# A two-layer hybrid decoder trunk on one core: first norm by plain transposes and a broadcast row of scales, transposed merge and gates, output in four banks, head 0 picked in halves, last two rows on VectorE

## The chip, the core and the metric
The kernel runs on one core of one Trainium2 chip. The metric is the device time of one launch in microseconds. Before the change it is 1635.47 us, the median of 3 runs (1634.2 to 1636.94). All data is float32.

## The reference
256 tokens of 1024 channels go through two equal layers and a last RMSNorm. A layer is:

```python
h = rmsnorm(x, g_mix)
p, q, k, v, gl = split(h @ w_in)                  # 512 | 512 | 512 | 512 | 2048
branch_a = pool_mixer(p, w_pool, pool_scale)      # trailing means over 2/4/8/16 tokens, minus the token,
                                                  # 4 groups of 128 channels mapped to 256 each, times pool_scale
o = moba_attention(q, k, v)                       # one block of 256: causal attention with ALiBi, 8 heads of 64
branch_b = o @ w_attn_up
gates = sigmoid(gl)
x = x + (gates[:1024] * branch_a + gates[1024:] * branch_b) @ w_out
x = x + peer_ffn(rmsnorm(x, g_ffn), ...)
```

`peer_ffn`: queries `xc @ w_q` (8 heads of 2 x 128), scores against 2 x 128 sub keys, the best 16 of each half, the best 16 of their 256 sums; so each token has 8 x 16 = 128 experts. Expert e adds `softmax weight * gelu(u[e] . xc) * v[e]`. The rows u[e] and v[e] lie side by side in one table `uv` (16384 per layer, 2048 floats each).

## The kernel before
**Tiles and windows.** The work is cut into four windows w = 0 to 3: layer w // 2, tokens of tile w % 2 (128 tokens, one a partition). Each window has two parts. The *mix* (`tensor_mix`, `scalar_mix`, `vector_mix`) is everything up to the choice of the experts: norm, projections, pooling, attention, gates, output projection, second norm, queries, scores and top 16. The *stream* is 64 ticks of two expert rows: GpSimd gathers one row per token (128 x 8 KB = 1 MB) into one of 8 ring slots; VectorE takes the dot product with `tok` (`dot`, L855); ScalarE makes the GELU weight and a diagonal matrix of it (`scalar_tick`, L667 to L692); TensorE adds diag @ v into two banks (`tensor_tick`, L514), or VectorE adds the row itself (`weighted`, L869). A slot is free for the next gather when its row is added.

**Order.** There is one hand-written order. `streamed` runs, on each engine, tick t of the stream and then the pieces of the mixes that are due at t; a mix piece says when with `yield when(w, n)`, which is tick 64 (w - 1) + 4 + n. So the mix of w + 1 runs inside the stream of w, and the mix of window 0 runs before tick 0, with nothing to stream. An engine executes its list in order and waits on semaphores in it.

**Weights.** They come in 30 chunks of 1 MB a window (`chunks`), issued by SyncE in order: C_Q and C_K (2 each), C_V, C_P (2 each), C_GATE (8), C_UP (2), C_OUT (4), C_PQ (8, one per PEER head). Chunks C_UP to the first of C_PQ are held in SBUF for both windows of a layer (`held`), the other 23 go through three slots (`wring`); SyncE waits until the chunk three before is used. In a tick in which a chunk of the next mix is due (`takes_chunk`), TensorE adds only row 1 and VectorE adds row 0. In window 0's own mix the chunks of the eight heads' queries are due at ticks -19, -17, ... -5.

**Banks.** Six PSUM banks are taken in turn by `claim(name, reader)`; TensorE waits until the bank six claims before has been read.

**The norm.** `squares` (ScalarE, L533), `inverse_mean` (VectorE, L707 and L709) and `root` (ScalarE, L537) give 1/rms per token; ScalarE turns it into a diagonal `rinv_diag` (L580); TensorE multiplies x by it, which transposes and scales at once (L391), and ScalarE copies the blocks to `hT` with the gain of each channel (`turned`, L544). Keys and gains arrive as rows and are transposed on TensorE (L384, L385).

**Pooling, gates, merge, output.** `everywhere` (L309) spreads a row of gains over all partitions; for `pool_scale` VectorE multiplies `wpool` by it (L802). `rows_by` (L355) makes results with the tokens on the partitions, `cols_by` (L373) with the channels. Gates, pooling and `up` (L470) have tokens on the partitions, so `merged` is made by VectorE (L810, L817, L821), transposed on TensorE (L328), copied by ScalarE (L524), and only then multiplied with the C_OUT chunks (L355) into two banks, which VectorE adds to x (L825). Then x is transposed again (L328) and copied with the second gain (L544).

**Heads.** For each head: queries (L373), copy (L524), scores (L493), copy, then on VectorE `key_search` (L722, L725, L728), `sum_search` (L738 to L749), `pick` (L755 to L766) and `weigh_heads` (L772, L774). GpSimd waits for `expert_ready` of a head before its first gather, `hand_over` (L847) makes `tok` at tick 0 of a window. After the last tick come `close` (L877) and the last norm of tile 1 (L895, L899, L908).

Of the kernel before, what the change touches and what calls it, by code (L numbers as in the profile page):

```python
# [20 lines left out]
P = 128  # L21
# [49 lines left out]
HEAD_LOADS = 5  # L71
# [10 lines left out]
G_MIX, G_FFN, G_POOL, G_FINAL = 0, KC, 2 * KC, 3 * KC  # L82
G_ROWS = 4 * KC
# [34 lines left out]
def build(nc, consts, chunks, uv, x, mix_norm, w_pool, pool_scale, ffn_norm, peer_keys, final_norm, out):  # L118
    depth = mix_norm.shape[0]
    windows = depth * NT  # L120

    with ExitStack() as ctx:
# [13 lines left out]
        gainT = sb("gainT", [P, 2, KC])  # L136
        wpool = sb("wpool", [P, NG, GOUT])
        keysT = sb("keysT", [P, 2, NK])
# [9 lines left out]
        rinv_diag = sb("rinv_diag", [P, P])  # L148
# [24 lines left out]
        keys = buf2[:, D:D + 2 * P].rearrange("p (a n) -> p a n", a=2)  # L173
# [20 lines left out]
        heads_in = sem("heads_in")  # L194
# [8 lines left out]
        rinv_diag_done = sem("rinv_diag_done")  # L203
# [18 lines left out]
        normed_done = sem("normed_done")  # L222
# [12 lines left out]
        def when(w, tick):  # L235
# [3 lines left out]
        first_heads = [(-10, -8, -6), (-2, -1, 1), (2, 3, 5), (7, 9, 10), (12, 13, 15), (17, 18, 20), (21, 23, 24),  # L239
                       (26, 27, 29)]  # L240

# [7 lines left out]
        takes_chunk = {when(w, n) for w in range(1, windows) for n in CHUNK_TICKS}  # L249

        def rows_on_tensor(t):

            return (1,) if t in takes_chunk else (0, 1)

# [58 lines left out]
        def tensor_mix(pe, w):  # L313
# [10 lines left out]
            def turn(name, half, src):  # L324
                b = claim(f"{name}{half}", a_done)
                for j in range(4):
                    lo = (4 * half + j) * P
                    ins = pe.transpose(b[:, j * P:(j + 1) * P], src[:, lo:lo + P], ident)  # L328
                filled(f"{name}{half}", ins)
# [13 lines left out]
            def due(c):  # L343
                return when(w, CHUNK_TICKS[c])
# [16 lines left out]
            def cols_by(c, name, n):  # L361
# [3 lines left out]
                for m in range(n):  # L365
# [4 lines left out]
                    for half in range(2):  # L370
                        lo = half * P
                        for k in range(KC):
                            ins = pe.matmul(b[:, m * CW + lo:m * CW + lo + P], wt[:, k, lo:lo + P], hT[:, k, :],  # L373
                                            start=(k == 0), stop=(k == KC - 1))
                freed[w, c + n - 1] = filled(name, ins)

            yield when(w, 3)
            if w == 0:
                pe.wait_ge(ident_in, 16)
            if tile == 0:  # L380
                pe.wait_ge(heads_in, 16 * HEAD_LOADS * (layer + 1))
                b = claim("heads", a_done)
                for a in range(2):
# [646 lines left out]
```

## Time and profile before
| what | value |
|---|---|
| median of 3 runs | 1635.47 us (1634.2 to 1636.94) |
| the profiled execution's own time | 1631.79 us |
| its span | 1630.0 us |
| busy PE / DVE / ACT / POOL | 1335.7 / 1078.0 / 772.2 / 615.3 us |
| moved by DMA | 653.33 MB, mean 401 GB/s |
| expert rows / weight chunks | 512 x 1 MB / 106 x 1 MB |
| mean granted TensorE clock | 0.957 |

The page gives each engine's busy time, the span in 40 equal slices, the DMA queues, the chain of work that ended last, and the costliest groups of instructions. PE is TensorE's matmul, PEld its weight load, DVE VectorE, ACT ScalarE, POOL GpSimd, SP SyncE; "L391" is line 391 of the kernel. A float32 product is recorded as two passes, so a query chunk of 16 products of 128 x 128 stands as x32; a transpose is one pass. The wait tables name for each idle time of an engine what ended it.

### The profile page before, as it was taken

What the parts mean: (1) busy time and instruction counts of PE and PEld (TensorE: products, weight loads), DVE (VectorE), ACT (ScalarE), POOL (GpSimd) and SP (SyncE); (2) the same over time, 40 slices, a digit from 0 to 9 for tenths busy, and PEclk for the clock granted to TensorE, in tenths of its full rate; (3) what the DMA queues carried; (4) which work ended last, traced back from release to release, by engine and by line L of the source; (5) the groups of instructions that cost most, each with busy time, mean ns of one, the idle gap of its engine ahead of it and who ended that gap; (6) DMA issues with size and microseconds to landing.
All of it is one profiled execution on the core that took longest, in us unless ns stands there. A gap on an engine that the chain in (4) does not pass through costs nothing.

```text
span 1630.0 us, 16753 instructions
## 1 busy us (share of the span) xinstructions
PE 1335.7 (82%) x4974; PEld 785.1 (48%) x4974; DVE 1078.0 (66%) x2539; ACT 772.2 (47%) x2882; POOL 615.3 (38%) x516
## 2 busy tenths in 40 slices
PE   8987878889878788877888888897988877778776
PEld 7876455535554265533454436563555422233322
DVE  0135879766678677755567787867656876777544
ACT  2223635445545544424554463544564555555554
POOL 0002432345434332323543343334543444554551
PEclk9998999999999898988999899999999999999999
DMA  7849999999999999999999999999999999999996
GB/s 290 305 183 387 412 423 410 424 422 414 421 423 411 423 402 423 422 426 417 416 420 423 415 400 410 423 423 422 415 422 422 413 421 421 421 413 421 402 421 250
DMA packets 91963, 653.33 MB, mean 401 GB/s; under 512 B 10144, under 2 KB 11872, under 8 KB 12768
## 3 DMA queue, kind: packets, MB, share of 16 engines
q0 software_dynamic: 73728, 536.90, 79.7%
q1 hardware_dynamic: 18144, 115.36, 17.4%
q8 instruction: 39, 0.64, 0.2%
q14 instruction: 52, 0.43, 0.1%
HBM read 651.17 MB, written 1.05 MB: 400 GB/s over the span
## 4 chain that ended last, share of the span: by engine, by line
DMA 51%; PE 19%; DVE 15%; issue 7%; ACT 5%; POOL 3%; another core or an unknown queue 0%; DVEq 0%; ACTq 0%; POOLq 0%
DMA ring<-in_uv,expert 50%; PE ybank L514 10%; DVE ring L855 6%; PE bank L373 3%; PE bank L355 3%; DVE xs L869 3%; POOL ring L953 3%; ACT wgt L681 1%; ACT diag L692 1%; ACT half_p L669 1%; ACT th L675 1%; DVE buf L758 1%; DVE picked L761 1%; DVE ci L728 1%; DVE buf L755 1%
## 5 line engine op out<-in xcount | busy, mean ns | idle before, releaser
L514 PE MATMUL ybank<-ring,diag 128*128 128x512 f32 x1688 | 834.1, 637 | 268.6 <-ACT diag L692 266.9
L953 POOL DMA_INDIRECT ring<-in_uv,expert x512 | 615.1, 1201 | 989.5 <-DVE xs L869 413.6
L855 DVE SCALAR_TENSOR_TENSOR ring<-ring,tok 128x1024 f32<-128x1024 f32 x512 | 620.4, 1224 | 402.9 <-DMA ring<-in_uv,expert 398.5
L514 PEld LDWEIGHTS ybank<-ring,diag 128*128 128x128 f32 x1688 | 317.6, 198 | 704.2 <-ACT diag L692 378.5
L667 ACT ACTIVATE sq<-dots 128x2 f32<-128x2 f32 x256 | 52.2, 204 | 704.7 <-DVE ring L855 704.7
L355 PE MATMUL bank<-wring,hT 128*128 128x256 f32 x768 | 178.1, 387 | 0.3 <-DMA wring<-in_chunks 0.3
L681 ACT ACTIVATE wgt<-th,half_p 128x1 f32<-128x1 f32 x512 | 170.1, 379 | 8.6
L355 PEld LDWEIGHTS bank<-wring,hT 128*128 128x128 f32 x768 | 150.8, 197 | 41.5 <-issue 21.3
L373 PEld LDWEIGHTS bank<-hT,wring 128*128 128x128 f32 x1408 | 164.7, 195 | 7.4 <-issue 5.7
L373 PE MATMUL bank<-hT,wring 128*128 128x128 f32 x1408 | 167.1, 278 | 1.2 <-ACT hT L544 1.2
L692 ACT ACTIVATE diag<-cst,wgt 128x128 f32<-128x128 f32 x422 | 149.8, 392 | 5.4
L669 ACT ACTIVATE half_p<-dots,prob 128x1 f32<-128x1 f32 x512 | 119.1, 280 | 0.0
L869 DVE SCALAR_TENSOR_TENSOR xs<-ring,wgt,xs 128x1024 f32<-128x1024 f32 x90 | 115.3, 1281 | 0.3 <-ACT wgt L681 0.3
L675 ACT ACTIVATE th<-arg,dots 128x1 f32<-128x1 f32 x256 | 75.4, 294 | 8.2
L672 ACT ACTIVATE arg<-sq,gelu_bias 128x2 f32<-128x2 f32 x256 | 71.9, 281 | 0.0
L676 ACT ACTIVATE th<-arg,dots 128x1 f32<-128x1 f32 x256 | 71.3, 279 | 0.0
L355 PE MATMUL bank<-held,hT 128*128 128x256 f32 x256 | 57.5, 379 | 0.7 <-ACT hT L524 0.7
L355 PEld LDWEIGHTS bank<-held,hT 128*128 128x128 f32 x256 | 48.6, 190 | 12.7 <-issue 5.7
L524 ACT ACTIVATE buf<-bank 128x256 f32<-128x256 f32 (+1 forms) x64 | 27.3, 448 | 55.0 <-PE bank L355 25.3
L855 DVE DVE_READ_ACCUMULATOR ring<-ring,tok 128x1 f32 x512 | 42.2, 82 | 0.0
L728 DVE FIND_INDEX8 si<-sv,buf 128x8 uint32<-128x128 f32 x128 | 34.9, 285 | 0.0
L725 DVE MAX8 sv<-buf 128x8 f32<-128x128 f32 x128 | 31.0, 284 | 5.4 <-ACT buf L524 4.3
(101 smaller groups left out, 702.0 us busy)
## 6 DMA issues: line engine op xcount, KB each, us to landing
wring<-in_chunks SPq DMA_DIRECT2D x92, 1024.0 KB
held<-in_chunks SPq DMA_DIRECT2D x14, 1024.0 KB, 17.3
ring<-in_uv,expert POOLq DMA_INDIRECT x512
xs<-in_x SPq DMA_DIRECT2D x2, 512.0 KB, 11.3
wpool<-in_w_pool SPq DMA_DIRECT2D x2, 512.0 KB, 14.0
trunk_out<-buf SPq DMA_DIRECT2D x4, 256.0 KB, 4.7
cst<-in_consts SPq DMA_DIRECT2D x1, 672.0 KB, 8.0
buf<-in_peer_keys SPq DMA_DIRECT2D x2, 128.0 KB
```

Of the source, the lines that this page charges most:

```text
L355: ins = pe.matmul(b[:, m * CW:(m + 1) * CW], hT[:, k, :], wt[:, k, :], start=(k == 0), stop=(k == KC - 1))
L373: ins = pe.matmul(b[:, m * CW + lo:m * CW + lo + P], wt[:, k, lo:lo + P], hT[:, k, :], start=(k == 0), stop=(k == KC - 1))
L514: ins = pe.matmul(ybank[m][:, :], diag[:, nth % DIAGS, :], ring[:, (2 * t + r) % RING, D + m * BANK:D + (m + 1) * BANK], start=(nth == ten ...
L669: act.activation(half_p[:, c:c + 1], dots[:, c:c + 1], ACT.Copy, scale=prob[:, w % 2, 2 * n + r:2 * n + r + 1])
L672: act_stepped(act.activation(arg[:, :], sq[:, :], ACT.Identity, scale=0.044715 * GELU_C, bias=gelu_bias[:, 0:1]))
L675: act.activation(th[:, 0:1], arg[:, 0:1], ACT.Tanh, scale=dots[:, col[0]:col[0] + 1])
L676: act_stepped(act.activation(th[:, 1:2], arg[:, 1:2], ACT.Tanh, scale=dots[:, col[1]:col[1] + 1]))
L681: ins = act.activation(wgt[:, c:c + 1], th[:, r:r + 1], ACT.Identity, scale=half_p[:, c:c + 1], bias=half_p[:, c:c + 1])
L692: act.activation(diag[:, nth % DIAGS, :], ident, ACT.Copy, scale=wgt[:, col[r]:col[r] + 1]).then_inc(diag_done, 1)
L855: dve.scalar_tensor_tensor(out=ring[:, g % RING, 0:D], in0=ring[:, g % RING, 0:D], scalar=1.0, in1=tok[:, :], op0=ALU.mult, op1=ALU.mult, ...
L869: dve.scalar_tensor_tensor(out=total, in0=ring[:, 2 * t % RING, D:2 * D], scalar=wgt[:, c:c + 1], in1=total, op0=ALU.mult, op1=ALU.add).th ...
L953: pool.indirect_dma_start(ring[:, g % RING, :], None, uv, bass.IndirectOffsetOnAxis(ap=expert[:, w % 2, at:at + 1], axis=0)).then_inc(row_ ...
```

## The change
- Mixing norm: TensorE transposes x as it is (no scaling), as soon as x is there. When 1/rms is ready, one product of `stat` broadcast over 128 columns with the identity gives a bank whose every row holds all tokens' scales; VectorE copies it (`rinv_all`) and makes `hT` with 8 `scalar_tensor_tensor` (block x gain x scale). ScalarE's `rinv_diag` and its 8 copies go. The first chunk's products wait for `hT` in two halves.
- Keys and gains come already transposed in one array (`side`, by `beside`); their transposes and copies go. In the SyncE list of window 0 chunk 0 is now ahead of them. `gains` has 3 rows of gains.
- `pool_scale` of layer 0 is a broadcast DMA into ring slot 0 (512 KB written), and VectorE multiplies `wpool` in one instruction; layer 1 still uses `everywhere`.
- Gates by `cols_by`, pooling and `up` with channels on the partitions, so `merged` is born transposed: its 8 transposes and 2 copies go. The factor 0.5 moves to the addition to x.
- Output in four banks of 256 columns, each added to x on its own tick (33 to 36). In window 0 the first four blocks of x are transposed ahead of the last C_OUT chunk.
- Window 0, head 0: query and score by side (a, b), the search of side a beside the product of side b; the squares of the second norm on VectorE; the 16 experts are picked in two halves of 8, and GpSimd starts after the first.
- Window 0's queries of heads 5, 6 and 7 move to ticks 0, 2 and 4; in these ticks row 0 goes to VectorE. `sum_search(1)` moves from tick -1 to tick 0; the weight of head 0 is made after `key_search(1)`.
- Last tick: both rows are added by VectorE, ScalarE makes their weights one after the other; the tensor sum is added ahead of the last row.
- Last norm: VectorE multiplies by the gain ahead of the root; then ScalarE scales columns 0 to 511 and VectorE the rest.

```diff
@@ order of window 0's queries
+        first_queries = (-19, -17, -15, -13, -11, 0, 2, 4)
+        def query_tick(w, h):
+            return when(w, CHUNK_TICKS[C_PQ + h]) if w else first_queries[h]
-        takes_chunk = {when(w, n) for w in range(1, windows) for n in CHUNK_TICKS}
+        takes_chunk = {when(w, n) for w in range(1, windows) for n in CHUNK_TICKS} | set(first_queries)
         def rows_on_tensor(t):
+            if t == windows * TICKS - 1:
+                return ()
             return (1,) if t in takes_chunk else (0, 1)
@@ tensor_mix: the norm
-            pe.wait_ge(rinv_diag_done, w + 1)
-            for half in range(2):
-                b = claim(f"h{half}", a_done)
-                for j in range(4):
-                    lo = (4 * half + j) * P
-                    ins = pe.matmul(b[:, j * P:(j + 1) * P], x_of(tile)[:, lo:lo + P], rinv_diag[:, :],
-                                    start=True, stop=True)
-                filled(f"h{half}", ins)
-            yield due(C_Q)
-            pe.wait_ge(*read(w, "h1"))
+            turn("h0", v_done, 0, 4)
+            turn("h1", v_done, 4, 4)
+            pe.wait_ge(root_done, 2 * w + 1)
+            b = claim("rinv", rinv_copied)
+            filled("rinv", pe.matmul(b[:, 0:P], stat[:, 0, 2:3].to_broadcast([P, P]), ident, start=True, stop=True))
@@ tensor_mix: head 0 of window 0
+            def first_query():
...
+                pe.wait_ge(x_mixed, OUTS * w + OUTS - 1)
+                g = claim("g2", a_done)
+                a = claim("pq0a", a_done)
+                side(0, a, range(6))
+                pe.wait_ge(x_mixed, OUTS * w + OUTS)
+                for j in range(2):
+                    ins = pe.transpose(g[:, j * P:(j + 1) * P], x_of(tile)[:, (6 + j) * P:(7 + j) * P], ident)
+                filled("g2", ins)
+                pe.wait_ge(*read(w, "g2"))
+                filled("pq0a", side(0, a, range(6, KC)))
+                a_scores, b = claim("score0a", a_done), claim("pq0b", a_done)
+                side(1, b, range(4))
+                scores(0, a_scores)
+                freed[w, C_PQ] = filled("pq0b", side(1, b, range(4, KC)))
+                scores(1, claim("score0b", a_done))
@@ tensor_mix: merge and output
-            yield when(w, 29)
-            pe.wait_ge(merged_done, 2 * (w + 1))
-            turn("merged", 0, merged)
-            turn("merged", 1, merged)
-            yield due(C_OUT)
-            pe.wait_ge(*read(w, "merged1"))
-            yield from rows_by(C_OUT, "out0", v_done)
-            yield from rows_by(C_OUT + 2, "out1", v_done)
+            for n in range(OUTS):
+                if w == 0 and n == OUTS - 1:
+                    turn_mixed(0)
+                yield due(C_OUT + n)
+                wt, b = weights(C_OUT + n), claim(f"out{n}", x_mixed)
+                for k in range(KC):
+                    if n == 0 and k % 4 == 0:
+                        pe.wait_ge(merged_done, 2 * w + k // 4 + 1)
+                    ins = pe.matmul(b[:, 0:CW], mergedT[:, k, :], wt[:, k, :], start=(k == 0), stop=(k == KC - 1))
+                freed[w, C_OUT + n] = filled(f"out{n}", ins)
@@ vector_mix: the norm
+            yield when(w, 4)
+            if tile == 0:
+                dve.wait_ge(side_in, 16 * (layer + 1))
+            dve.tensor_copy(rinv_all[:, :], bank("rinv")[:, 0:P]).then_inc(rinv_copied, 1)
+            dve.wait_ge(*read(w, "rinv"))
+            for half in range(2):
+                b = bank(f"h{half}")
+                for j in range(4):
+                    k = 4 * half + j
+                    ins = dve.scalar_tensor_tensor(out=hT[:, k, :], in0=b[:, j * P:(j + 1) * P],
+                                                   scalar=gainT[:, 0, k:k + 1], in1=rinv_all[:, :],
+                                                   op0=ALU.mult, op1=ALU.mult)
+                ins.then_inc(v_done, 1)
@@ the last tick and the last norm
+        def close_last(dve):
+            w, t = windows - 1, windows * TICKS - 1
+            weighted(dve, t, 0).then_inc(dve_summed, 1)
+            dve.wait_ge(dve_summed, vector_rows(t) + 1)
+            dve.wait_ge(pe_summed, tensor_rows(t))
+            for m in range(2):
+                step(sum_of_tensor(dve, w, m))
+            settle(dve)
+            weighted(dve, t, 1).then_inc(x_final, 2)
...
+            act.activation(normed(tile)[:, 0:BANK], normed(tile)[:, 0:BANK], ACT.Copy,
+                           scale=stat[:, tile, 2:3]).then_inc(normed_a, 1)
...
+            dve.tensor_scalar(normed(tile)[:, BANK:D], normed(tile)[:, BANK:D], stat[:, tile, 2:3], None,
+                              ALU.mult).then_inc(normed_v, 1)
@@ gathers and SyncE's list
-                    if at % TOPK == 0:
-                        pool.wait_ge(expert_ready, PH * w + at // TOPK + 1)
+                    if g == 0:
+                        pool.wait_ge(expert_ready, 1)
+                    elif g == 8:
+                        pool.wait_ge(expert_ready, 2)
+                    elif at % TOPK == 0:
+                        pool.wait_ge(expert_ready, experts_of(w, at // TOPK))
...
+                        if tile == 0 and c == (1 if w == 0 else 0):
+                            heads(layer)
                         chunk(w, c)
...
+                            if layer == 0:
+                                sp.dma_start(ring[:, 0, 0:D], pool_scale[0:1, :].to_broadcast([P, D])
+                                             ).then_inc(scale_in, 16)
```

## Rows read from the trace of the kernel before

**Rows 1.** The page: DMA share in tenths and GB/s in 40 slices.
```profile
DMA  7849999999999999999999999999999999999996
GB/s 290 305 183 387 412 423 410 424 422 414 421 423 411 423 402 423 422 426 417 416 420 423 415 400 410 423 423 422 415 422 422 413 421 421 421 413 421 402 421 250
```

**Rows 2.** Stretches of the whole core: length, busy (count) by engine, clock, DMA share, GB/s.
```profile
95.00:111.00 16.00, 13.86 (x96) 12.50 (x95) 3.06 (x15) 4.27 (x13) 0.00 (x0) 1.00 0.01 3
...
155.00:160.00 5.00, 5.00 (x10) 2.13 (x9) 4.83 (x21) 3.73 (x14) 1.88 (x2) 0.78 0.38 123
...
200.00:1600.00 1400.00, 1144.40 (x4012) 642.97 (x4011) 991.66 (x2287) 691.10 (x2625) 582.02 (x484) 0.96 1.01 418
```

**Rows 3.** Chain that ended last, window 0's mix: start us, us, what.
```profile
6.29 3.80 PE bank L391 x16
...
10.11 1.15 ACT hT L544 x4
...
11.31 11.00 PE bank L373 x96
22.32 7.26 DMA wring<-in_chunks
...
49.44 1.98 PE bank L309 x16
...
76.16 6.88 PE bank L470 x16
...
86.44 14.08 PE bank L355 x64
...
100.99 2.19 ACT hT L544 x8
...
103.22 3.85 PE bank L373 x32
```

**Rows 4.** VectorE's instructions from head 0's search to its pick.
```profile
108.85 0.49 DVE L725 MAX8 sv<-buf 128x8 f32<-128x128 f32 x2 [4.26 <-ACT buf L524]
...
118.44 0.17 DVE L766 TENSOR_SCALAR expert<-picked 128x16 uint32<-128x16 f32 x1
```

**Rows 5.** Groups of VectorE instructions by shape, whole run.
```profile
L786 DVE SCALAR_TENSOR_TENSOR buf<-cst,bank 128x128 f32<-128x128 f32 x16 | 3.8, 280 | 28.6 <-PE bank L406 28.6
...
L869 DVE SCALAR_TENSOR_TENSOR xs<-ring,wgt,xs 128x1024 f32<-128x1024 f32 x90 | 115.3, 1281 | 0.3 <-ACT wgt L681 0.3
```

**Rows 6.** GpSimd's gathers: start, us, [idle before <- what ended it].
```profile
118.90 1.08 POOL L953 DMA_INDIRECT ring<-in_uv,expert  x1 [118.44 <-DVE expert L766]
...
127.74 1.30 POOL L953 DMA_INDIRECT ring<-in_uv,expert  x1 [0.30 <-issue]
156.55 0.94 POOL L953 DMA_INDIRECT ring<-in_uv,expert  x1 [27.50 <-PE ybank L514]
```

**Rows 7.** Waits in 118 to 135 us, the longest of ScalarE.
```profile
ACT buf L524 <- remote: 6.9, 1, 6.9
```

**Rows 8.** A stretch of the mix of window 1 inside stream 0, columns as in rows 2.
```profile
260.00:270.00 10.00, 7.14 (x21) 4.18 (x20) 9.76 (x24) 4.17 (x18) 2.23 (x2) 0.84 1.02 420
```

**Rows 9.** The last ticks and the end, all engines in order of time.
```profile
1603.29 1.74 POOL L953 DMA_INDIRECT ring<-in_uv,expert  x1 [0.76 <-PE ybank L514]
...
1614.18 3.70 PE L514 MATMUL ybank<-ring,diag 128*128 128x512 f32 x8 [1.27 <-ACT diag L692]
...
1615.39 1.23 DVE L855 SCALAR_TENSOR_TENSOR ring<-ring,tok 128x1024 f32<-128x1024 f32 x1 [1.23 <-DMA ring<-in_uv,expert]
...
1619.12 3.70 PE L514 MATMUL ybank<-ring,diag 128*128 128x512 f32 x8 [1.24 <-ACT diag L692]
...
1622.92 1.29 DVE L877 TENSOR_TENSOR xs<-xs,ybank 128x512 f32<-128x512 f32 x2 [6.30 <-PE ybank L514]
1624.24 1.06 ACT L895 ACTIVATE buf<-xs 128x1024 f32<-128x1024 f32 x1 [3.38 <-DVE xs L877]
...
1626.05 1.41 DVE L908 SCALAR_TENSOR_TENSOR buf<-xs,stat,bank 128x512 f32<-128x512 f32 x2 [0.27 <-ACT stat L899]
```

More of the change, by code:

```diff
@@ L375, in cols_by, with side, scores @@
                 freed[w, c + n - 1] = filled(name, ins)
+            def first_query():
+                wt = weights(C_PQ)
+                def side(r, b, ks):
+                    for k in ks:
+                        ins = pe.matmul(b[:, 0:P], wt[:, k, r * P:(r + 1) * P], hT[:, k, :],
+                                        start=(k == 0), stop=(k == KC - 1))
+                    return ins
+                def scores(r, b):
+                    pe.wait_ge(*read(w, f"pq0{'ab'[r]}"))
+                    filled(f"score0{'ab'[r]}", pe.matmul(b[:, 0:NK], pqT[:, r, :], keysT[:, r, :],
+                                                         start=True, stop=True))
+                pe.wait_ge(x_mixed, OUTS * w + OUTS - 1)
[13 more added lines that the diff above has]
+                scores(1, claim("score0b", a_done))
             yield when(w, 3)
@@ L485, in tensor_mix @@
+            yield when(w, 37)
+            if w:
+                turn_mixed(0)
+            turn_mixed(1)
+            if w:
+                turn_mixed(2)
             yield due(C_PQ)
             pe.wait_ge(*read(w, "g1"))
-            for h in range(PH):
+            if tile == 0:
+                pe.wait_ge(side_in, 16 * (layer + 1))
+            if w == 0:
+                first_query()
+            else:
+                pe.wait_ge(*read(w, "g2"))
+            for h in range(0 if w else 1, PH):
@@ L488, in tensor_mix @@
                 yield from cols_by(C_PQ + h, f"pq{h}", 1)
-                yield when(w, 43 + 2 * h)
+                if w == 0 and h == 1:
+                    pe.wait_ge(gains_in, 16)
+                    everywhere(pe, w, G_FFN, "gain")
+                yield query_tick(w, h) + 2
                 pe.wait_ge(*read(w, f"pq{h}"))
@@ L495, in tensor_mix @@
                 filled(f"score{h}", ins)
-                if w == 0 and h == 1:
-                    everywhere(pe, w, G_FFN, "gain")
             if w:
@@ L620, in scalar_mix @@
             yield when(w, 30)
-            for half in range(2):
-                copy_out(f"merged{half}", hT[:, 4 * half:4 * half + 4, :], scale=0.5)
             if w == 0:
```

383 lines of the change are left out of this document (228 added, 155 removed).

## The prediction
> **What bounds the kernel now.** I read the slices first [rows 1]. There are two regimes. In the first three slices (to 122 us) DMA moves 290, 305 and 183 GB/s; from the fourth on it stays near 420 with a busy share of 9 tenths, to the last slice. The stretches say the same more finely [rows 2]: 200 to 1600 us runs at 418 GB/s with a DMA share of 1.01, while TensorE is busy 1144 of 1400 us and VectorE 992. So the stream is bound by transfers: 512 rows and the chunks must pass, and what an engine saves in it is worth nothing by itself. Between 95 and 111 us DMA stands still (share 0.01): everything that fits is loaded, and no expert is known yet. The first gather goes at 118.90, released by the experts of head 0 [rows 6]. So what counts is (1) how early the gathers begin, (2) idle DMA after that, (3) the time from the last row's landing (1615.39, when VectorE's wait for it ends [rows 9]) to the end of the span, 1630.0: 14.6 us.
>
> In the chain [rows 3] the reader is to see that window 0's mix is bound by TensorE, with short stops in which another engine works on what TensorE waits for. Those stops are what the change goes for. I take the sum against the profiled execution (span 1630.0, its own time 1631.79, which is 3.7 under the median 1635.47) and move the difference to the median.
>
> **First norm.** Before, the first projection starts at 11.31: x scaled on TensorE from 6.29 to 10.09, four copies on ScalarE, start [rows 3]. After, the eight transposes need only x and the identity and lie beside the squares on ScalarE; the root is done at about 5.8 (the diagonal's use starts at 6.29, 0.45 behind it). Then one product (2 passes, 0.5), a copy and 4 VectorE instructions on 128 x 128 from a bank. Such a one takes 280 ns alone [rows 5], about 0.24 in a series: 1.3 for the first half, so TensorE could start at 7.7, and the second half comes 1.0 later, beside 8 passes of the first products. That saves 3.6. Against it: VectorE first waits for `side`, which SyncE issues behind 1.6 MB of x and chunk 0; at the rates of the start that is near 7.0 to 7.5, so the start moves to about 8.5. And TensorE: its 16 passes at 6.29 took 3.80, 0.237 each, the 96 from 11.31 on 11.00, 0.115 each [rows 3]: it works at half speed until it has worked a while, that is at 1.2 of its two levels 1.2 and 2.4 GHz. The new kernel gives it less to do before the first projection, so part of chunk 0 may run slow: up to 1.8 (half of its 3.6). Bounds: saves 0.3 to 3.6; I take 2.0.
>
> The Trainium skill ("TensorE: Matmul & The Clock Gate", Part 1) says the same of it: the throttled clock is the default and activity releases it. The row agrees (0.237 against 0.115); by that rule alone the saving would be 3.6 - 0.8 - 1.8 = 1.0 and not 2.0, which is the second rival below.
>
> **Scale of the pool.** `everywhere` for it stands in the chain with 1.98 [rows 3]; in layer 0 it goes. VectorE's multiplication lies beside gate chunks. The broadcast DMA writes 0.5 MB at a time when SyncE's chunks are just in time (chunk 5 took 7.26 from issue to use [rows 3]): 0.5 MB at 0.42 MB/us is 1.2. Bounds: saves 0.8 to 2.0; I take 2.0: the chunks of 30 to 95 us have room, DMA stands still from 95 on [rows 2].
>
> **Up to output.** `up` ends at 83.04 (76.16 + 6.88) and the output product starts at 86.44 [rows 3]: 3.4 of VectorE, transposes and copies. After, the first half of `merged` is ready 1.5 after `up0`, so under `up1`; the second is ready 1.5 after `up1`, while the first four blocks of out0 take 8 passes of 128 x 256, 1.8 (16 such passes are a chunk, 3.5). Nothing is left of the stop: 3.3 saved, bounds 2.9 to 3.4. The same products as channels by tokens cost as much (32 passes at 0.112 against 16 at 0.22). Four transposes of x go ahead of the last output chunk: +0.6.
>
> So the last output product ends at 100.5 - 2.0 - 2.0 - 3.3 + 0.6 = 93.8.
>
> **From there to the first gather.** Before: 118.9 - 100.5 = 18.4: 2.7 to the query product (ScalarE's 8 copies, 2.19), 3.85 for it [rows 3], copies and scores to 108.85, search and pick to 118.44 (9.8) [rows 4]. After, counted from the end of the last output product E: g1 copied, TensorE goes on at E + 1.15; 12 passes 1.35; two transposes and copies, E + 3.9; 4 passes, a copy (4.7), 8 passes of side b meanwhile, score a and its copy E + 5.9; search a 1.8, E + 7.7. Side b: passes, copy, score, copy, also E + 7.7; search b, E + 9.5. Sums 0.55, best 8 and places 1.45, pick of 8: six instructions of 128 x 128 at 0.31 and two small, 2.25; E + 13.7, and 0.4 to GpSimd: 14.1. Saved 4.3; bounds 2 (copies and waits pile up) to 5.5. First gather at about 107.9, 11.0 earlier.
>
> **What lies behind it.** Moving the gathers does not move all bytes. The chunk of head 4 (1 MB), loaded by 118.9 before, is now issued only 3 ahead of the first gather: +1.5. The stream then starts with 8 rows and 4 chunks, some 28 us of transfer. Before, TensorE did the queries of heads 5 to 7 first; no slot came free until 156.55 [rows 6], and DMA ran dry: share 0.38 in 155 to 160 [rows 2], 3.5 with its edges. After, TensorE reaches tick 0 at about 119.5 (five queries, the gain bank) and the first slots come free at 124: cover 107 to 134, so 10 to spare, and the dry stretch goes: -3.5. The spare also covers ScalarE's one odd wait of 6.9 [rows 7], should it return. Bounds 0 to 3.5.
>
> **In the stream.** VectorE gets more: three rows for heads 5 to 7 (3 x 1.28 [rows 5]); in each mix a copy, 8 instructions (2.3) and, new, a wait for TensorE. Behind that wait in VectorE's list are the dots of the next tick. VectorE is a tick ahead: TensorE ends tick 3 about 6.8 after its dots (ScalarE 3, TensorE 3.7), the transposes and the product add 1.6, so VectorE waits 3.4 and is back 5.7 later, 3.3 behind the rows. A gather issued at 1603.29 is used at 1615.39 [rows 9], 12.1 later, of which a row's own transfer is 2.5 and the fixed part about 2: 7.6 of slack. It holds. But in window 0's stream VectorE has places without any (9.76 busy of 10 [rows 8]). Bounds 0 to 6; I take 2, nearer to the slack of rows 9. What ScalarE and TensorE lose there is worth 0.
>
> Last row used at 1615.4 - 11.0 + 1.5 - 3.5 + 2.0 = 1604.4.
>
> **The end.** Before, from the landing L: dot 1.25, ScalarE, TensorE 3.7 from L + 3.7, sums (1622.92), squares, root, two products with the gain, the second ready at L + 12.1, output [rows 9]. After: TensorE's last work is tick 254's, L - 1.2 + 3.7 = L + 2.5; sums 1.3; last row on VectorE 1.25: L + 5.1 against L + 8.8. Its weight is there at L + 2.6. Squares 1.2 beside 1.4 of gain, inverse 0.4, root 0.2, then 0.6 on ScalarE beside VectorE: L + 7.9; output 2.5 and 0.4 for a second issue: 10.8 instead of 14.6, -3.8, bounds 2.5 to 4.5.
>
> **Sum.** -11.0 + 1.5 - 3.5 + 2.0 - 3.8 = -14.8: span 1615.2, median 1635.5 - 14.8 = 1620.7.
>
> **Rivals.**
> 1. VectorE or TensorE sets the pace of the first 150 us of stream 0 and the early start runs into full slots: the 3.5 stay and the stream costs 6 instead of 2, -7.3: 1628.2. For it: VectorE at 9.76 of 10 [rows 8]. Against: DMA share 1.02 in that same row.
> 2. The first projection runs at 1.2 GHz for its first 3.6 (the passes of 0.237 in rows 3): the start gives 1.0 instead of 2.0, 1621.7.
> 3. Slower: VectorE's new wait isn't covered. Place: tick 4 of each mix in the stream; price: 5.7 in each of three windows, 17.1, and the three added rows 3.8: 20.9 in the place of my 2.0, 1639.6. It decides once the slack of 7.6 falls under 3.3. Against: rows 9's own gap.
> 4. The change does no more than shift the gathers: chunks that could be loaded early are behind them, and in place of 1.5 the first rows share DMA with 4 chunks until VectorE starves: 5 of the 11.0 is lost, 1625.7.
> 5. Everything goes to its good bound (3.6, 5.5, no loss in the stream, 4.5): 1615.2.
>
> **Chances.** Forecast 0.47, rival 1 0.16, rival 2 0.12, rival 3 0.05, rival 4 0.11, rival 5 0.09. The range of 8 in 10 is 1613.5 to 1629.0. A measurement of this kernel can tell some 0.2% (3.3 us) from no change. Faster by more: 0.90 (all but rival 3 and the tail of rival 1); within it 0.05; slower 0.05.
>
> **What would show it.** The first product of the first projection at 8 to 9 us; the output product right behind `up`; no `everywhere` before 100; the first gather at 106 to 110; DMA share above 0.95 in every 5 us from 110 on; tick 0's first product at 120 to 124; last landing to end 11. I am wrong if DMA runs dry in the first 60 us of the stream or the rate in the stream falls under 415.

## The result and the profile after
The changed kernel takes 1620.24 us (median of 4, 1619.65 to 1624.07) against 1634.84 (median of 4, 1632.85 to 1636.94); the ratio is 0.9919 [0.9908, 0.9931]. 1620.7 was forecast. The number is right and part of its sum is not: the start gave less than half of what I counted (5.2 of 11.0), and executions of one kernel differ by more (up to 8 us) than the error of 5.8 that this left.

The first two fences are the page of the changed kernel, its two lines of 40 slices, and stretches of it (length, busy by engine, clock, DMA share, GB/s), to be laid beside [rows 1] and [rows 2].

```profile
DMA  7859999999999999999999999999999999999996
GB/s 289 305 232 423 399 422 420 423 422 421 420 422 410 415 389 424 422 424 419 413 421 423 413 409 400 422 424 421 419 413 424 410 414 422 421 418 417 411 422 285
```
```profile
95.00:111.00 16.00, 14.11 (x105) 12.82 (x103) 7.57 (x30) 4.16 (x14) 0.00 (x0) 1.00 0.09 30
...
155.00:160.00 5.00, 3.21 (x15) 1.96 (x15) 1.23 (x2) 2.53 (x11) 1.48 (x2) 1.00 1.01 426
...
200.00:1600.00 1400.00, 1145.56 (x4511) 669.59 (x4509) 995.52 (x2305) 684.92 (x2605) 564.45 (x484) 0.95 1.01 417
```

The empty stretch 95 to 111 is still empty. The dry one at 155 to 160 is gone (share 0.38 before, 1.01 now). The stream's rate is the same: 417 against 418.

The start, against [rows 3]: TensorE, then VectorE (start, us, instructions, idle before and what ended it), then the first projection's passes alone in two single microseconds.

```profile
4.31 1.97 PE L364 MATMUL bank<-cst,xs 128*128 128x128 f32 x8 [4.31 <-DMA cst<-in_consts]
6.07 0.66 PE L463 MATMUL bank<-cst,stat 128*128 128x128 f32 x2
11.64 16.75 PE L416 MATMUL bank<-hT,wring 128*128 128x128 f32 x128 [4.91 <-DVE hT L904]
28.23 7.07 PE L396 MATMUL bank<-wring,hT 128*128 128x256 f32 x32
```
```profile
10.04 0.29 DVE L898 COPY rinv_all<-bank 128x128 f32<-128x128 f32 x1 [4.39 <-DMA beside<-in_side]
10.37 2.16 DVE L904 SCALAR_TENSOR_TENSOR hT<-bank,beside,rinv_all 128x128 f32<-128x128 f32 x8
```
```profile
12.00:13.00 1.00, 1.00 (x6) 1.00 (x6) 1.00 0.58 246
...
17.00:18.00 1.00, 1.00 (x12) 1.00 (x11) 1.00 0.00 0
```

The transposes are done at 6.3, but VectorE waits 4.39 for `beside` (the SBUF copy of the array `side`), which lands 7.9 after its issue. The first projection starts at 11.64, not before the 11.31 of [rows 3], and does 6 passes in the microsecond from 12 but 12 in the one from 17: by its passes it begins at the lower of the two levels, 1.2 GHz. The clock column doesn't show it: it reads 1.00 in both, as it does for the slow passes of [rows 3].

The way to the gathers, against [rows 3, 6], and the end, against [rows 9]:

```profile
60.19 1.95 PE L516 MATMUL bank<-qT,wpool 128*128 128x128 f32 x16
...
77.48 7.31 PE L540 MATMUL bank<-qT,held 128*128 128x128 f32 x64
84.63 2.65 PE L551 MATMUL bank<-held,buf 128*128 128x256 f32 x11
```
```profile
113.67 1.08 POOL L1123 DMA_INDIRECT ring<-in_uv,expert  x1 [113.22 <-DVE expert L859]
...
137.13 0.94 POOL L1123 DMA_INDIRECT ring<-in_uv,expert  x1 [12.67 <-DVE xs L1014]
```
```profile
1610.03 3.70 PE L597 MATMUL ybank<-ring,diag 128*128 128x512 f32 x8 [1.28 <-ACT diag L775]
...
1611.25 1.22 DVE L1001 SCALAR_TENSOR_TENSOR ring<-ring,tok 128x1024 f32<-128x1024 f32 x1 [1.23 <-DMA ring<-in_uv,expert]
...
1613.84 1.28 DVE L1020 TENSOR_TENSOR xs<-xs,ybank 128x512 f32<-128x512 f32 x2 [0.16 <-PE ybank L597]
...
1615.22 1.28 DVE L1014 SCALAR_TENSOR_TENSOR xs<-ring,wgt,xs 128x1024 f32<-128x1024 f32 x1
...
1616.55 1.06 ACT L1055 ACTIVATE buf<-xs 128x1024 f32<-128x1024 f32 x1 [1.19 <-DVE xs L1014]
...
1618.36 0.72 ACT L1062 ACTIVATE buf<-buf,stat 128x512 f32<-128x512 f32 x1
```

The output product follows `up` at once (84.63). The first gather goes at 113.67 (118.90 before), the ninth at 137.13 (156.55 before). From the last landing, 1611.25, to the end of the span, 1622.3, it is 11.05 against 14.6.

### The profile page after: what moved, and what is told of

Same layout as the page of the kernel before. It is cut to its first block and busy times, and to the rows that moved or that the text cites. A ratio compares the mean times of both kernels' runs of the same rounds, so it can differ in the third digit from the quotient of the medians.

```text
span 1622.3 us, 18071 instructions
## 1 busy us (share of the span) xinstructions
PE 1323.5 (82%) x5612; PEld 814.4 (50%) x5612; DVE 1098.2 (68%) x2602; ACT 756.4 (47%) x2833; POOL 597.5 (37%) x516
## 5 line engine op out<-in xcount | busy, mean ns | idle before, releaser
L747 ACT ACTIVATE sq<-dots 128x2 f32<-128x2 f32 (+1 forms) x257 | 52.2, 203 | 732.4 <-DVE ring L1001 732.3
L416 PEld LDWEIGHTS bank<-hT,wring 128*128 128x128 f32 x2432 | 291.6, 198 | 27.1 <-issue 27.1
L416 PE MATMUL bank<-hT,wring 128*128 128x128 f32 x2432 | 293.0, 281 | 4.9 <-DVE hT L904 4.9
L757 ACT ACTIVATE th<-arg,dots 128x1 f32<-128x1 f32 x512 | 122.9, 287 | 8.2
L753 ACT ACTIVATE arg<-sq,gelu_bias 128x2 f32<-128x2 f32 (+1 forms) x257 | 72.0, 280 | 0.0
L396 PE MATMUL bank<-wring,hT 128*128 128x256 f32 x256 | 58.6, 383 | 0.4 <-DMA wring<-in_chunks 0.4
L551 PE MATMUL bank<-held,buf 128*128 128x256 f32 x256 | 57.7, 379 | 0.0
L396 PEld LDWEIGHTS bank<-wring,hT 128*128 128x128 f32 x256 | 49.0, 193 | 13.3 <-issue 6.3
L551 PEld LDWEIGHTS bank<-held,buf 128*128 128x128 f32 x256 | 48.4, 190 | 11.8 <-issue 5.7
L607 ACT ACTIVATE buf<-bank 128x256 f32<-128x256 f32 (+2 forms) x65 | 27.4, 443 | 41.6 <-PE bank L416 34.6
```

The source lines that it names most:

```text
L396: ins = pe.matmul(b[:, m * CW:(m + 1) * CW], hT[:, k, :], wt[:, k, :], start=(k == 0), stop=(k == KC - 1))
L551: ins = pe.matmul(b[:, 0:CW], mergedT[:, k, :], wt[:, k, :], start=(k == 0), stop=(k == KC - 1))
L753: act_stepped(act.activation(arg[:, these], sq[:, these], ACT.Identity, scale=0.044715 * GELU_C, bias=gelu_bias[:, 0:1]))
L757: ins = act.activation(th[:, r:r + 1], arg[:, r:r + 1], ACT.Tanh, scale=dots[:, col[r]:col[r] + 1])
```

## The experiments
Times are medians, each with its ratio to the kernel before measured beside it on the same chip. Behind the first comparison, whose chip isn't on record, three chips were used: a1 and e1 to e3 ran on one (the kernel before has 1634.22 there), b1 and e4 to e6 on a second (1635.12), a2, b2, e7 and e8 on a third (1629.35). Where two medians of different chips are compared, the ratios are the safer measure. For each profiled execution I read three points: the first gather, the last row's use (as 1615.39 in [rows 9]), the end of the span.

| kernel | median | ratio [95%] | span | first gather | ninth | first gather to last row | last row to end |
|---|---|---|---|---|---|---|---|
| before | 1634.84 | 1 | 1630.0 | 118.90 | 156.55 | 1496.5 | 14.6 |
| before again (b1) | 1632.04 | 0.9988 [0.9976, 1.0001] | 1631.5 | 120.10 | 158.45 | 1496.8 | 14.6 |
| before again (b2), another chip | 1629.03 | 0.9998 [0.9989, 1.0007] | 1625.9 | 118.60 | 152.49 | 1492.7 | 14.7 |
| changed | 1620.24 | 0.9919 [0.9908, 0.9931] | 1622.3 | 113.67 | 137.13 | 1497.6 | 11.1 |
| changed again (a1) | 1621.08 | 0.9917 [0.9899, 0.9936] | 1619.4 | 114.36 | 138.05 | 1494.0 | 11.0 |
| changed again (a2), b2's chip | 1620.43 | 0.9952 [0.9939, 0.9966] | 1616.9 | 113.19 | 139.40 | 1492.7 | 11.0 |
| e1 side first | 1619.99 | 0.9910 [0.9889, 0.9930] | 1618.7 | 112.61 | 136.00 | 1495.0 | 11.1 |
| e2 and early products | 1617.00 | 0.9895 [0.9875, 0.9916] | 1612.2 | 108.11 | 133.10 | 1493.0 | 11.1 |
| e3 old end | 1625.60 | 0.9945 [0.9924, 0.9967] | 1622.3 | 113.44 | 138.08 | 1494.3 | 14.6 |
| e4 old query ticks | 1627.46 | 0.9958 [0.9944, 0.9972] | 1629.0 | 115.03 | 156.65 | 1502.8 | 11.1 |
| e5 scalar norm in the stream | 1618.96 | 0.9909 [0.9893, 0.9925] | 1617.0 | 113.89 | 138.26 | 1492.1 | 11.0 |
| e6 head 0 whole | 1620.82 | 0.9923 [0.9909, 0.9937] | 1617.3 | 115.44 | 137.88 | 1490.9 | 11.0 |
| e7 side, early products, scalar norm, b2's chip | 1614.31 | 0.9909 [0.9894, 0.9924] | 1611.9 | 107.97 | 132.57 | 1492.9 | 11.1 |
| e8 forty more on ScalarE, b2's chip | 1604.58 | 0.9851 [0.9835, 0.9866] | 1601.7 | 113.57 | 138.80 | 1477.1 | 11.0 |

**The changed kernel again (a1).** No edit. 

> The changed kernel, unaltered. The result so far has a gain of 14.6 us between medians, but only 7.7 between the two profiled executions (1630.0 to 1622.3 of span); the sum of the changed kernel's trace, step by step, explains 7.7 plus or minus 3. If the stream differs by chance from execution to execution (417 against 418 GB/s is 3 us over 1400 us), a new profiled execution lies near 1618 of span with the first gather at the same 113.7 and the same 11.0 from the last landing to the end. If something in the start is what varies, the first gather moves.

Span 1619.4, first gather 114.36, and 1494.0 between them instead of 1497.6: what varies is the stream, by 3.6 with one and the same code, and hardly the start (0.7).

**Keys and gains ahead of chunk 0 (e1).**
```diff
+                        if w == 0 and c == 0:
+                            sp.dma_start(beside[:, :], side[0]).then_inc(side_in, 16)
-                        if tile == 0 and c == (1 if w == 0 else 0):
-                            heads(layer)
```
(The gains' rows stay behind chunk 0, layer 1 as it was.) 

> The changed kernel with the array of keys and gains issued ahead of chunk 0 instead of behind it. Theory A (the array's landing at 10.0, 7.9 after its issue, holds the first projection): it lands near 6.5 to 7, the first product goes to 8.5 to 9 from 11.64, and the first gather comes some 2.5 earlier than 113.7, the time is 2.5 less than the changed kernel's. Theory B (TensorE's slow level sets the end of the first projections, so an earlier start only makes more of it slow): the third chunk's products end at most 1 earlier. Rival C (the transfers of chunks set the pace up to 45 us): VectorE gets its gains early, but waits for chunks appear and nothing is left at the output product.

Its TensorE:

```profile
9.16 17.30 PE L416 MATMUL bank<-hT,wring 128*128 128x128 f32 x128 [2.36 <-DMA wring<-in_chunks]
26.30 7.08 PE L396 MATMUL bank<-wring,hT 128*128 128x256 f32 x32
...
39.34 3.72 PE L396 MATMUL bank<-wring,hT 128*128 128x256 f32 x16 [1.12 <-DMA wring<-in_chunks]
```
```profile
6.91 0.29 DVE L898 COPY rinv_all<-bank 128x128 f32<-128x128 f32 x1 [1.20 <-PE bank L463]
```

VectorE now copies the scales at 6.91, after a wait of 1.20 for TensorE's product and none for the array. The first product moves from 11.64 to 9.16, where it waits for chunk 0. But the stretch that took 16.75 takes 17.30, and a wait of 1.12 for a chunk appears at 39.34 (0.42 before). Of 2.5 at the first product, 1.9 are left at 26.30 (28.23), 1.1 at the output product (83.56 against 84.63), 1.1 to 1.8 at the first gather, 1.1 in the median, which is less than the medians can tell. Theory A holds for the start. Of what was to come of it B and C each took a part and neither holds as it was put: the first 128 passes end 1.9 earlier (B had at most 1), and something is left at the output product (C had nothing).

**And products of zeros ahead of the first projection (e2).** As e1, and
```diff
+        def warm_up(pe, n):
+            for _ in range(n):
+                pe.matmul(banks[5][:, 0:P], diag[:, 0, :], diag[:, 0, :], start=True, stop=True)
...
+                pe.wait_ge(bias_set, 2)
+                warm_up(pe, 7)
...
+            if w == 0:
+                warm_up(pe, 7)
...
+                dve.memset(diag[:, 0, :], 0.0).then_inc(bias_set, 1)
```
(Seven products ahead of the transposes of window 0, seven behind the product of the scales.) 

> As the last one, and TensorE does 7 products of zeros before x lands and 7 more between the row of scales and the first projection (their results are overwritten). Theory: the first projection then runs at 0.115 a pass and not at 0.15 to 0.24; it gains another 2.0 to 2.3 over the last kernel, so 4.5 to 5 in all. Rival: chunk 1 and 2 haven't landed and TensorE waits for them instead; it gains under 1 over the last kernel.

```profile
1.09 3.35 PE L351 MATMUL bank<-diag 128*128 128x128 f32 x14 [1.09 <-DVE diag L1108]
...
6.45 1.96 PE L351 MATMUL bank<-diag 128*128 128x128 f32 x14
8.72 14.56 PE L420 MATMUL bank<-hT,wring 128*128 128x128 f32 x128 [0.32 <-DMA wring<-in_chunks]
23.12 7.07 PE L400 MATMUL bank<-wring,hT 128*128 128x256 f32 x32
```
```profile
108.11 1.08 POOL L1132 DMA_INDIRECT ring<-in_uv,expert  x1 [107.66 <-DVE expert L867]
```

The first 14 passes take 3.35 (0.24 each), the 14 at 6.45 take 1.96 (0.14 each), and the first projection's 128 take 14.56 instead of 17.30, as many as from 11.31 to 25.87 before the change. The first gather is at 108.11, 4.5 earlier than in e1 and as early as my sum had it (107.9). Of the 4.5, 3.2 are there when C_V starts (23.12 against 26.30), and 0.8 more are a shorter wait for a chunk (0.36 against 1.12). The median is 3.0 lower than e1's; the intervals of the two ratios overlap, so it is the trace that shows this step. It is the second rival's mechanism. The Trainium skill, "TensorE: Matmul & The Clock Gate" (Part 1), has it that the throttled clock is the default and activity releases it; the passes agree (0.24 in a TensorE that had stood idle, 0.114 in one that had done the products of zeros).

**The old end (e3).** Undoes the last tick on VectorE, `close_last`, and the order of the last norm. 

> The changed kernel with the old end: last tick's rows on TensorE, its close, and the last norm in the old order. My sum has 3.8 for this part, the traces 14.6 against 11.05 from the last landing, 3.6. Expected: 3.4 to 3.8 slower than the changed kernel, all of it behind the last landing. Rival: the last landing moves too.

1625.60 against 1621.08 on the same chip: 4.5. In the profiled executions the last row is used at 1607.72 and the span ends 14.6 later (1622.3), against 11.0: 3.6. The first gather is the same. So the term is 3.6 by the trace; the rest of 4.5 lies within the spread of its runs (1621.4 to 1629.3).

**The queries of heads 5 to 7 ahead of tick 0 (e4).**
```diff
-        first_queries = (-19, -17, -15, -13, -11, 0, 2, 4)
+        first_queries = (-19, -17, -15, -13, -11, -9, -7, -5)
-        takes_chunk = {when(w, n) for w in range(1, windows) for n in CHUNK_TICKS} | set(first_queries)
+        takes_chunk = {when(w, n) for w in range(1, windows) for n in CHUNK_TICKS}
```
(`sum_search(1)` at tick -1.) 

> The changed kernel with the queries of heads 5 to 7 at their old ticks -9, -7, -5, so ahead of tick 0, no rows of ticks 0, 2, 4 on VectorE, and sum_search(1) at tick -1 again. My sum has 3.5 for the dry stretch of DMA: the ninth gather goes near 150 and not at 137, DMA is at a share of about 0.4 for 5 us before 155, and the time is 3 to 4 longer than the changed kernel's. Rival: with the transfers of more chunks behind the eight rows nothing runs dry and the time is the same; or VectorE's relief in the first ticks makes it up, within 1.

```profile
115.03 1.07 POOL L1123 DMA_INDIRECT ring<-in_uv,expert  x1 [114.58 <-DVE expert L859]
...
156.65 0.94 POOL L1123 DMA_INDIRECT ring<-in_uv,expert  x1 [31.83 <-PE ybank L597]
```
```profile
115.00:160.00 45.00, 34.31 (x218) 29.12 (x217) 25.24 (x89) 14.69 (x47) 9.53 (x10) 0.89 0.86 339
```

Now GpSimd waits 31.83 for its ninth slot, and 115 to 160 runs at 339 GB/s; two executions of the changed kernel (a1 and the first) have 401 and 407. 45 us at (407 - 339) / 423 is 7.2, a part of which is the first gather that comes 0.7 to 1.4 later. The dry stretch alone, 148 to 160, has a share of 0.56, against 0.74 in the kernel before: some 5.3 us of empty DMA against 3.2. The median is 6.4 above a1's (6.7 by the ratios: 0.9958 - 0.9917 = 0.0041 of 1634) and 6.6 above that of e6, which ran beside it. The stretch between the first gather and the last row is 5.2 to 8.8 longer, but the profiled execution is the slowest of its six (1630.76). So the step is worth nearly twice what I had. The dry stretch is set by two ends, and the change moves the first gather forward while the ninth, with the old ticks, stays at 156.65: the stretch would have grown.

**The first norm of windows 1 to 3 on ScalarE (e5).** For w > 0 the diagonal (`ACT.Copy` of the identity times the scale), L391's products and the 8 ScalarE copies as in the kernel before. 

> The changed kernel with the first norm of windows 1 to 3 as before the change (diagonal on ScalarE, scaling on TensorE, copies on ScalarE); window 0 keeps the new one. My sum took 2 of loss (0 to 6) for VectorE's added wait and work in the stream, the slower rival 5.7 a window. If the ring's slack covers it the time is the changed kernel's within 1; if not, it is 2 to 6 shorter, with the stretch from first gather to last landing shorter by that.

What it takes away, in the changed kernel, and 180 to 200 us in both:

```profile
183.28 0.29 DVE L898 COPY rinv_all<-bank 128x128 f32<-128x128 f32 x1 [3.36 <-PE bank L463]
```
```profile
180.00:200.00 20.00, 16.28 (x71) 9.83 (x71) 16.14 (x45) 7.29 (x30) 6.67 (x6) 0.91 0.97 394
```
```profile
180.00:200.00 20.00, 18.84 (x103) 12.94 (x101) 17.27 (x41) 11.38 (x47) 6.36 (x7) 1.00 1.01 421
```

VectorE's wait for TensorE was foretold with 3.4 and is 3.36. There DMA falls to a share of 0.97 and 394 GB/s; with the norm on ScalarE it is 1.01 and 421: 20 us at 27 / 423 is 1.3. Over 180 to 220 it is 397 in the changed kernel and 402 in a1, against 423: 2.5 and 2.0. So in these executions the loss is near the 2.0 of the sum. It isn't there in all: VectorE's wait is 3.36 to 3.37 in the changed kernel, a1 and e1 (388 to 394 GB/s in 180 to 200), 2.2 to 2.4 in e2, e3, e6 and e8 (409 to 419), and 1.26 in a2 (419). Outside window 1 it is small (560 to 600 us: 381 and 388 against 394). That taking it away shortens the kernel is not shown: the median is 2.1 under a1's, from another chip, and 1.9 under e6's, but the ratios are 0.9909, 0.9917 and 0.9923, and their intervals overlap. The slower rival, which wanted 20.9, is out.

**Head 0's experts picked whole (e6).**
```diff
-                for lo in (0, 8):
-                    ...
-                    places(these)
-                    pick_of(0, lo, 8, hot)
+                sum_search(0)
+                pick(0)
```


> The changed kernel with head 0's 16 experts picked in one go (searches by side are kept). From the rows, sums 0.55, two searches 2.5, places 0.5, pick 3.2 make 6.75 against 4.25: the first gather goes 2.5 later, at 116.5, and the time grows by 2 to 2.5. Rival: the whole pick is done 1.8 sooner than both halves, so head 0's weight and the first dots come earlier, and what is lost at the first gather is made up in part: under 1.

```profile
115.44 1.07 POOL L1110 DMA_INDIRECT ring<-in_uv,expert  x1 [114.99 <-DVE expert L859]
...
137.88 0.94 POOL L1110 DMA_INDIRECT ring<-in_uv,expert  x1 [11.69 <-DVE xs L1001]
```

The first gather is 1.1 to 2.3 later (2.5 expected), the ninth is where it was, and the time is the same (0.9923 against 0.9917 and 0.9919). The rival's size (under 1) was right, its reason was not: the first dot product starts at 122.91, no earlier than in the changed kernel (122.43, a1 123.12). From 105 to 138 DMA moves 303 GB/s here, 304 in the changed kernel and 297 in a1. By the ninth gather as many bytes are through in either case, so the halves bring the first rows forward and win nothing with it.

**The parts that helped, together (e7).** e2 and e5. 

> The parts that helped, together: keys and gains ahead of chunk 0, the early products of zeros on TensorE, and the first norm of windows 1 to 3 on ScalarE as before the change. If they add: 1621.1 less 4.1 (first two) less 1.5 to 2 (third) is 1615 to 1615.5, with the first gather at 108 and the stretch to the last landing near 1491 to 1493. Rival: both work on the same slack of the first ticks of the stream, and the third brings nothing more: 1617.

1614.31, 6.1 under the changed kernel's 1620.43 on the same chip (ratios to before 0.9909 and 0.9952), and 0.7 to 1.2 under the 1615 to 1615.5 of the sum of the parts. The number is as if they added, the trace says otherwise: against a2 the first gather is 5.2 earlier (107.97) and the stretch behind it is the same (1492.9 and 1492.7). So the gain is the start's, and of the third part nothing is seen here; a2 has no dip at 180 to 200 that it could mend. The rival's mechanism isn't excluded.

**Forty more instructions on ScalarE (e8).**
```diff
+        padding = sb("padding", [P, 40])
             if w == 0:
                 act.activation(warm[:, 1:2], gelu_bias[:, :], ACT.Sqrt)
+                for n in range(40):
+                    act.activation(padding[:, n:n + 1], gelu_bias[:, :], ACT.Copy)
```


> The changed kernel with 40 small copies more on ScalarE in its idle time between 78 and 95 us. In each kernel so far ScalarE stands still for 5.5 to 6.9 us, ended by nothing the profile can name, just as the first gathers begin, although the product it waits for is done 4 us earlier. Theory: it waits for its own next instructions, whose load is behind the rows; then the stop comes 40 instructions sooner, in the stretch in which DMA is empty, and is gone or short; TensorE gets to tick 0 4 to 6 earlier (the ninth gather at 132 and not 137) and the time is 0 to 2 less. Rival: it belongs to that copy or to its bank, and stays at 5.5 in its place.

The same 50 us in e8, then in a2:

```profile
1530.00:1580.00 50.00, 37.32 (x81) 14.67 (x82) 25.26 (x42) 26.81 (x103) 27.29 (x21) 1.00 1.01 427
```
```profile
1530.00:1580.00 50.00, 37.18 (x81) 14.55 (x82) 24.78 (x42) 26.29 (x102) 28.11 (x21) 1.00 1.01 422
```

For the question it was made for it says nothing, because on this chip the stop isn't there in the changed kernel either (next paragraph). It shows something else: 1604.58, 15.9 under the changed kernel and 24.8 under the kernel before, and no step of the start differs (first gather 113.57). The rate does: 427 against 422 GB/s here, and 421, 420 and 425 in 260 to 600, 600 to 1000 and 1000 to 1500, against 415, 417 and 420. In the last ticks, in which VectorE waits for each row, rows come every 2.453 us (mean of 20 or more steps from 1530 to 1580) in e8, and every 2.484 to 2.486 in e7 and all six executions of the two kernels (2.483 to 2.487 in e1 to e4 and e6). 512 rows at 0.031 are 15.9, the whole gain. I see no way from forty copies at 80 us to a row at 1550. What else the edit does is to put 160 bytes a partition ahead of the tensors declared after `warm`, the ring among them; the change itself left the ring where it was (1088 bytes of keys and gains before and after). That the ring's start is the cause was not tried by itself: the forty instructions also move what follows them in ScalarE's program.

**The changed kernel on that chip (a2).** 

> The changed kernel once more, as the yardstick of this call. The same stretches as in the two profiled executions: first gather at 113.7 to 114.4, 1494 to 1497.6 to the last landing, 11.0 from there.

1620.43 against 1629.35 for the kernel before: a gain of 8.9 and not 13. The two profiled executions of this chip, b2 and this one, add up to the same: first gather -5.4, from there to the last row 0.0, the end -3.6, together -9.0. The kernel before moved, not the changed one. In all other profiled executions ScalarE has the stop of [rows 7] (6.9; 7.6 in b1; 5.8 in the changed kernel, 3.7 to 5.7 in e1 to e6), here in none of the four kernels:

```profile
125.21 0.39 ACT L607 ACTIVATE buf<-bank 128x256 f32<-128x256 f32 x1 [5.76 <-remote]
```
```profile
120.37 0.38 ACT L607 ACTIVATE buf<-bank 128x256 f32<-128x256 f32 x1 [1.38 <-PE bank L416]
```

The first line is the changed kernel's, the second a2's; both are the same copy in ScalarE's list. In the kernel before the stop lies ahead of tick 0 with nothing to cover it, so its ninth gather is at 152.49 without it and at 156.55 and 158.45 with it; the changed kernel has its ninth at 137 to 139 either way.

**The kernel before on that chip (b2)** and **on another (b1).** 

> The kernel before once more. Its two profiled executions (1630.0, 1631.5 of span) both lie at the fast end of 1631 to 1639. If an execution of 1635 or more is profiled, the stretch from first gather to last landing (1496.5 and 1496.8 so far) takes the difference; if it is fast again, that stretch is 1496 to 1497 and the question stays open.

 

> The kernel before, unaltered, for a second profiled execution of it: its runs spread over 8 us (1631.0 to 1639.3) and the one profiled lies at the fast end. If the spread lies in the stream, the first gather is again at 118.9 and the last landing to end 14.6, and only the stretch between them, 1496.5, differs, by up to 7. If it is in the start, the first gather moves.

b2: 1629.03, the stretch 1492.7. b1: the start is as expected, 1496.8 between; 1632.04 in 10 executions, while the same code in 17 more executions on that chip has 1635.12. No execution of 1635 or more was profiled. What makes them longer stays open. In b2, without ScalarE's stop, there is something else to see. The 12 us around the ninth gather in the profile of [rows 2], then in b2:

```profile
148.00:160.00 12.00, 8.58 (x25) 4.31 (x25) 6.19 (x23) 8.72 (x34) 1.88 (x2) 0.86 0.74 294
```
```profile
144.00:156.00 12.00, 8.58 (x23) 4.06 (x22) 6.80 (x25) 8.72 (x34) 1.87 (x2) 0.86 1.01 425
```

The kernel before has no dry stretch there, although its queries of heads 5 to 7 lie ahead of tick 0 as before: the ninth gather comes at 152.49, before DMA is empty. So the dry stretch of [rows 2] takes two things, the order of the queries and, as it seems, ScalarE's stop. Where the stop is absent there is no dry stretch to take away; the moved queries only keep the earlier first gather from opening one. That fits the 8.9 of this chip. What brings the stop was not found, and it was not switched on or off by itself.

## Why the prediction was right, and where it was not
Step by step, forecast and measured (profiled executions):

| step | forecast | measured |
|---|---|---|
| first norm, to the start of C_V (25.70) | -2.0 | +2.5 |
| from there to the pool's products (`everywhere` gone, 59.23) | -2.0 | -1.6 |
| to the end of `up` (83.04) | 0 | +0.6 |
| stop between `up` and output (3.4) | -3.3 | -3.4 |
| output and the four transposes | +0.6 | +0.5 |
| last output product to first gather (18.4) | -4.3 | -3.9 |
| first gather | -11.0 | -5.2 (-4.5 in a1) |
| first gather to last row | 0 (1.5 - 3.5 + 2.0) | +1.1 (-2.5 in a1) |
| the end | -3.8 | -3.6 |
| sum | -14.8 | -7.7 (-10.6 in a1); medians -14.6, -13.1, -8.9 |

**Wrong: the first norm.** The step that failed is "I take 2.0": it had both mechanisms and too small a size for each. `side` came at 10.0 and not at 7.0 to 7.5, so the first product started at 11.64 and not at 8.5. The slow passes cost 2.2 (the first 128 passes take 16.75 against 14.56), where I had up to 1.8 and counted less than half of it. Both in full at my sizes would have been 1.0 saved (the second rival); measured is 2.5 lost. e2 takes both away and gets 5.1 back at C_V. My lower bound of 0.3 saved was 2.8 off.

**Missed: more and smaller passes cost a little more.** A pair of gate chunks takes 7.31 as 64 passes of 128 x 128 and 7.07 to 7.17 as 32 of 128 x 256, `up` 7.31 as 64 passes against 7.03 as 16 of 128 x 512. I called them equal. It is 0.6 in the third row of the table.

**Right: the stop at the output, the search by sides, the end,** each within 0.4. The output follows `up`; e3 has 3.6 for the end.

**Right in the net, wrong in its parts: the stretch after the first gather.** The dry stretch goes. Moving the queries is worth 6.4 by the medians of e4 and not 3.5, since the stretch would have grown; e4 was measured only with ScalarE's stop of [rows 7], which I had as something the spare would cover. The stop seems to be a part of what made the stretch dry: in b2, without it, the share is 1.01 around the ninth gather, and the stretch from first gather to last row is 1492.7 in both kernels. TensorE reaches tick 0 at 135.48 (129.79 in a2) and not at 119.5, and the ninth gather goes at 137 to 139 and not at 124; the spare of 10 wasn't there. VectorE's 2.0 was of the right kind (e5: 2.0 to 2.5, and almost nothing in a2). The 1.5 for head 4's chunk was not measured by itself. The halves of head 0 are in my 4.3 and bring nothing in the time (e6). That a first gather earlier by x ends the kernel earlier by x, as the sum has it, does not hold for each part of x.

**How the total came out.** 5.8 too much at the start stand against the difference between profiled and other executions of the kernel before: the three profiled have own times of 1631.8, 1633.3 (b1) and 1627.7 (b2, where the kernel's are 1626.8 to 1631.7), at the short end of the 1631 to 1639 of the other chips. So the agreement of 1620.24 with 1620.7 is in part luck: the traces, which compare execution with execution, give 3.6 to 14.6 by which of them are paired, and 9.0 for the one pair of one chip (b2 and a2). Of the rivals, the second (slow TensorE) was true in its mechanism, though it still had 1.0 saved where 2.5 were lost; the third (slower) is refuted by e5; the first and fourth by the DMA share of 1.00 between 115 and 160 with 407 GB/s, except for the dip at 180 to 220. Two sums of the prediction don't come out: the fourth rival's 5 in place of 1.5 gives 1624.2, and 8 rows and 4 chunks at 2.484 are 30 us of transfer and not 28. Of its signs, the output product, the absent `everywhere` and the 11 of the end were met. The first product (11.64), the first gather (113.67), tick 0 and a DMA share above 0.95 in every 5 us (0.59 in 110 to 115, 0.89 in 115 to 120, 0.84 in 195 to 200) were not.

## What to carry to other kernels
When transfers bound the body of a kernel, look for the two ends of each empty stretch of DMA: what fills it and what frees the next slot; moving only one end moves the stretch. A stretch can be dry because of a stop that only some executions have, so profile the kernel before more than once, and on more than one chip. Work given to another engine early on is worth what its last input allows: here a 140 KB array behind a 1 MB chunk held the first product back by 2.5 us, and TensorE's slow passes cost 2 more, which fourteen products of zeros gave back. Before tuning instructions in a stream of transfers, measure the rate of one row, and again after each edit: in e8 it was 1.2% better for a reason that stays open, and that was more than this whole change.

## What the runs showed of the hardware
- One and the same stream of 1 MB gathers ran at 2.483 to 2.487 us a row in twelve executions, of both kernels, e1 to e4, e6 and e7, and at 2.453 in e8, whose edit shifts the later tensors by 160 bytes a partition (and adds 40 instructions). The cause was not separated.
- ScalarE stood still for 3.7 to 7.6 us as the first gathers began, ended by nothing in the profile, in all ten other executions profiled, and not at all in the four on the third chip. The granted clock in 125 to 130 us, in which the stop ends, is 0.65 in the kernel before and 0.66 in the changed one. From the first gather to the ninth the kernel before takes 33.9 without the stop and 37.7 and 38.4 with it, the changed one 26.2 without and 23.5 and 23.7 with it.
- A `scalar_tensor_tensor` on 128 x 128 from a bank with a scalar per partition and a second SBUF operand is recorded with 343 ns and starts every 0.26 us in a series of eight, against the 280 ns of [rows 5].
- The kernel before spreads by up to 8 us in 27 executions on one chip (1630.9 to 1638.9). None of the long ones was profiled. Two executions of the changed kernel differ in the stream (1497.6 and 1494.0) and hardly in the start and the end.
